# Moving the modulation sums of a hybrid layer kernel: second gate's sums into the experts' second product, one sum a level in the delta rule's inverse

## The reference, cut to what matters

```
mod = silu(c) @ w_ada + b_ada              # c: one row of 1024, w_ada: 1024 x 6144
shift1, scale1, gate1, shift2, scale2, gate2 = split(mod, 6)
h = rms_norm(x, norm1_gain) * (1 + scale1) + shift1
... h @ w_in, banded attention, convolution ...
# gated delta rule, per chunk of 64 tokens and head:
sol = triangular_solve(I + lower, rhs)     # unit lower triangular, here by its inverse
x = x + gate1 * (mix @ w_out)
h = rms_norm(x, norm2_gain) * (1 + scale2) + shift2
y = peer(h)     # 16384 one-neuron experts: gelu(h @ down), routed gates, (gates * act) @ up
x = x + gate2 * y
```

## Time and profile before

| | |
|---|---|
| median of 3 runs | 1708.43 us (1706.43 to 1713.17) |
| the profiled execution | 1703.49 us, its span 1701.8 us |
| PE busy | 1583.1 us, 93% |
| DVE busy | 1240.0 us, 73% |
| ACT busy | 899.9 us, 53% |
| granted PE clock, mean | 0.971 |
| DMA | 314.37 MB, mean 185 GB/s |

### The profile page before, as it was taken

The page is one execution under the profiler, slowest core; times in us unless marked ns, Lnnn a source line. Parts: engine busy times, 40 slices in busy tenths (PEclk is TensorE's granted clock), DMA queues, the critical chain, the costliest instruction groups (busy, mean ns, idle before and its releaser), DMA issues. The chain is left out here.

```text
span 1701.8 us, 26523 instructions
## 1 busy us (share of the span) xinstructions
PE 1583.1 (93%) x10358; PEld 1431.5 (84%) x10358; DVE 1240.0 (73%) x2494; ACT 899.9 (53%) x1497; POOL 45.6 (3%) x83
## 2 busy tenths in 40 slices
PE   5985789899999999999999999899999898989988
PEld 5975668899999999988888888797888677789977
DVE  5887777789997999956777766657886666654654
ACT  6763255455545555545555555556556746454443
POOL 0002300000000000000000000020000000000000
PEclk9997889999999999999999999999999899999999
DMA  9953446476766545557777767654443222545542
GB/s 327 336 178 96 150 169 197 134 238 225 227 210 224 167 145 167 157 194 249 243 245 247 240 237 242 209 174 149 142 153 127 73 76 100 173 148 174 188 156 102
DMA packets 110809, 314.37 MB, mean 185 GB/s; under 512 B 8465, under 2 KB 9057, under 8 KB 101217
## 3 DMA queue, kind: packets, MB, share of 16 engines
q1 hardware_dynamic: 98976, 276.94, 48.9%
q10 hardware_dynamic: 11040, 33.66, 5.8%
q0 software_dynamic: 672, 2.12, 0.4%
HBM read 293.80 MB, written 18.89 MB: 184 GB/s over the span
## 5 line engine op out<-in xcount | busy, mean ns | idle before, releaser
L300 PE MATMUL ps<-parts,parts 128*128 128x512 f32 (+1 forms) x4992 | 971.5, 356 | 27.2 <-DVE parts L290 21.0
L300 PEld LDWEIGHTS ps<-parts,parts 128*128 128x128 f32 x4992 | 824.6, 191 | 162.0 <-DVE parts L290 20.1
L285 ACT CAST parts<-lead 128x512 fp32r<-128x512 f32 x940 | 579.3, 620 | 624.6 <-PE ps L300 399.1
L290 DVE TENSOR_TENSOR parts<-lead,parts 128x512 fp32r<-128x512 f32 x940 | 641.1, 688 | 341.0 <-ACT parts L285 337.7
L1742 PE MATMUL ps<-parts,parts 128*128 128x256 f32 x3072 | 386.8, 285 | 4.5 <-DVE parts L290 4.5
L1742 PEld LDWEIGHTS ps<-parts,parts 128*128 128x128 f32 x3072 | 374.1, 192 | 5.5 <-DVE parts L290 5.5
L375 PE MATMUL ps<-lead,mem 128*128 128x128 f32 (+2 forms) x292 | 47.2, 328 | 50.7 <-ACT mem L491 25.9
L375 PEld LDWEIGHTS ps<-lead,mem 128*128 128x128 f32 (+2 forms) x292 | 41.4, 164 | 56.6 <-ACT mem L491 27.4
L1916 DVE TENSOR_SCALAR mem<-lead,mem 128x128 f32<-128x128 f32 x256 | 71.0, 339 | 0.0
L1728 PE MATMUL ps<-mem 128*128 128x128 f32 x512 | 67.8, 275 | 0.7 <-DVE mem L1916 0.7
L1728 PEld LDWEIGHTS ps<-mem 128*128 128x128 f32 x512 | 62.8, 192 | 1.1 <-issue 1.1
(11 more groups left out here) (339 smaller groups left out, 968.5 us busy)
## 6 DMA issues: line engine op xcount, KB each, us to landing
lead<-in_peer_expert_down SPq DMA_DIRECT2D x64, 1024.0 KB, 5.6
lead<-in_peer_expert_up SPq DMA_DIRECT2D x64, 1024.0 KB, 5.6
lead<-in_w_in SPq DMA_DIRECT2D x50, 1024.0 KB, 5.1
lead<-in_w_ffn_in SPq DMA_DIRECT2D x22, 1024.0 KB, 5.1
act_spill<-mem ACTq DMA_DIRECT2D x32, 512.0 KB, 5.1
mem<-act_spill ACTq DMA_DIRECT2D x32, 512.0 KB, 3.5
mem<-in_w_ada SPq DMA_DIRECT2D x27, 512.0 KB, 5.3
lead<-in_w_ffn_out SPq DMA_DIRECT2D x11, 1024.0 KB, 4.9
```

The costliest lines, as they stand in the source:

```text
L285: act.copy(w_hi[g % BUFFERS], st.words(n, u * UNIT, UNIT)).then_inc(hi_ready, 1)
L290: dve.tensor_tensor(w_lo[g % BUFFERS], st.words(n, u * UNIT, UNIT), w_hi[g % BUFFERS].bitcast(F32), ALU.subtract).then_inc(lo_ready, 1)
L300: mm = pe.matmul(o, lhs[a], rhs[b], start=start and i == 0, stop=stop and i == 2, skip_group_check=True, **kw)
```

## The change

Three things move.
- The second gate's eight sums leave the inverse, w_out and the query product. They are now made in the experts' second product, one behind unit 7 of each of the groups 20 to 27 (`late_mod`). Their tiles are loaded into pieces 4 to 11 of the gates: SP waits until `weights(11)` is done (`s_pr` 12) and then issues one tile behind every second weight piece (`load_late`). The columns' bias is added behind unit 228, and only then can POOL store the gate and load the row.
- The other 24 fills are dealt anew: two behind level 0 of the inverse as before, one behind each of levels 1 to 5, one behind the copy of line 1399, four in w_out.
- The bias, shift and scale of the second norm are formed in w_out, behind units 12 and 13.

The row silu(c) now lies in the place of the second gate's row (`gate2`), since it must last until group 27 and the gate's row comes after.

```diff
-        c_row = at(O_MODS + 3 * D, D)
+        c_row = gate2
...
-        FILL1, FILL2, FILL3, FILL4 = 9, 12, 25, 32
-        fill_tile = [f % FILLS if f < FILL3 else (f - FILL3) % (FILLS - 1) for f in range(FILL4)]
+        FILL1, FILL2, FILL3, FILL4 = 9, 12, 20, 24
+        fill_tile = [f % FILLS for f in range(FILL4)]
+        late_tiles = [at(O_R + (4 + i) * D, D) for i in range(KT)]
...
+        def load_late(sp, i):
+            sp.dma_start(late_tiles[i], A["w_ada"][(5 * KT + i) // 2][:, i % 2 * D:(i % 2 + 1) * D]).then_inc(s_late, 16)
+        def late_mod(dve, i):
+            if i == 0:
+                dve.wait_ge(s_late, 16 * KT)
+            v = late_tiles[i]
+            dve.scalar_tensor_tensor(out=v, in0=v, scalar=1.0, in1=c_row, op0=ALU.mult, op1=ALU.mult,
+                                     accum_out=mod_cols[:, 5 * KT + i:5 * KT + i + 1]).then_inc(s_mod, 1)
...
-                    fill_mods(dve, FILL2 + 2 * i, FILL2 + 2 * i + 2)
+                    fill_mods(dve, FILL2 + i + (i > 0), FILL2 + i + 2)
...
-                dve.wait_ge(s_mod, 3 * KT)
-                cols = mod_cols[:, 3 * KT:5 * KT]
-                dve.tensor_tensor(cols, cols, mod_bias[:, 3 * KT:5 * KT], ALU.add).then_inc(s_gate, 1)
-                dve.wait_ge(s_gain, 48)
-                dve.wait_ge(s_gate, 2)
-                dve.tensor_copy(norm_shift, cols[:, 0:KT])
-                dve.scalar_tensor_tensor(out=norm_scale, in0=cols[:, KT:2 * KT], scalar=1.0, in1=gain_cols[:, 1, :],
-                                         op0=ALU.add, op1=ALU.mult)
-                fill_mods(dve, FILL2 + 12, FILL3)
+                fill_mods(dve, FILL2 + 7, FILL3)
...
         def mods_beside_rows(dve, i):
             if i in (5, 7, 9, 11):
                 fill_mods(dve, FILL3 + (i - 5) // 2, FILL3 + (i - 3) // 2)
+            elif i == 12:
...
+                dve.tensor_tensor(cols, cols, mod_bias[:, 3 * KT:5 * KT], ALU.add).then_inc(s_gate, 1)
+            elif i == 13:
...
+                dve.tensor_copy(norm_shift, mod_cols[:, 3 * KT:4 * KT])
+                dve.scalar_tensor_tensor(out=norm_scale, in0=mod_cols[:, 4 * KT:5 * KT], scalar=1.0, in1=gain_cols[:, 1, :],
+                                         op0=ALU.add, op1=ALU.mult)
...
-                    if c and u == 1:
-                        fill_mods(dve, FILL4 - 4 + c, FILL4 - 3 + c)
-                    if c == 3 and u == 5:
-                        gates = mod_cols[:, 5 * KT:6 * KT]
-                        dve.wait_ge(s_mod, FILL4)
-                        dve.tensor_tensor(gates, gates, mod_bias[:, 5 * KT:6 * KT], ALU.add).then_inc(s_gate, 1)
...
+                st.issue(sp, n_up[0] + 24)
+                sp.wait_ge(s_pr, 12)
+                for i in range(KT):
+                    load_late(sp, i)
+                    st.issue(sp, n_up[0] + 26 + 2 * i)
                 st.issue(sp, n_in2a[0])
...
+                    if i % 8 == 7 and 20 <= q < 20 + KT:
+                        late_mod(dve, q - 20)
+                    if i == 8 * 28 + 4:
+                        gates = mod_cols[:, 5 * KT:6 * KT]
+                        dve.wait_ge(s_mod, 4 * KT)
+                        dve.tensor_tensor(gates, gates, mod_bias[:, 5 * KT:6 * KT], ALU.add).then_inc(s_gate, 1)
```

More of the change, by code:

```diff
@@ L422, in build @@
         fill_tiles = [at(o, D) for o in fill_at]
-        FILL1, FILL2, FILL3, FILL4 = 9, 12, 25, 32
-        fill_tile = [f % FILLS if f < FILL3 else (f - FILL3) % (FILLS - 1) for f in range(FILL4)]
+        FILL1, FILL2, FILL3, FILL4 = 9, 12, 20, 24
+        fill_tile = [f % FILLS for f in range(FILL4)]
+        late_tiles = [at(O_R + (4 + i) * D, D) for i in range(KT)]
         fill_before = [max((e for e in range(f) if fill_tile[e] == fill_tile[f]), default=None) for f in range(FILL4)]
+        s_late = lasting_sem("late_tiles_loaded")
         s_fill = [lasting_sem(f"fill_loaded{i}") for i in range(FILLS)]
@@ L1276, in _ @@
             def _(sp):
-                load_fills(sp, FILL2 + FILLS, FILL4 - 3)
+                load_fills(sp, FILL2 + FILLS, FILL4)
             @block.gpsimd
@@ L1521, in mods_beside_rows @@
                 fill_mods(dve, FILL3 + (i - 5) // 2, FILL3 + (i - 3) // 2)
+            elif i == 12:
+                cols = mod_cols[:, 3 * KT:5 * KT]
+                dve.wait_ge(s_mod, 3 * KT)
+                dve.tensor_tensor(cols, cols, mod_bias[:, 3 * KT:5 * KT], ALU.add).then_inc(s_gate, 1)
+            elif i == 13:
+                dve.wait_ge(s_gain, 48)
+                dve.wait_ge(s_gate, 2)
+                dve.tensor_copy(norm_shift, mod_cols[:, 3 * KT:4 * KT])
+                dve.scalar_tensor_tensor(out=norm_scale, in0=mod_cols[:, 4 * KT:5 * KT], scalar=1.0, in1=gain_cols[:, 1, :],
+                                         op0=ALU.add, op1=ALU.mult)
         rows_stage("w_out", n_wout, 4, n_query[0] + SLOTS, (x_hi, x_lo), add_mix, Turn("mix1", mix), sum_roots,
-                   last=lambda sp: load_fills(sp, FILL4 - 3, FILL4), beside=mods_beside_rows)
+                   beside=mods_beside_rows)
         first_sems = retired()
```

## The result

The changed kernel takes 1714.66 us (median of 12 runs, 1707.68 to 1719.2) where the kernel before takes 1709.28 us beside it (12 runs, 1704.3 to 1713.88): a ratio of 1.003 with an interval of [1.0016, 1.0044]. Run once more later it took 1717.3 us beside 1708.05, a ratio of 1.0052 [1.0032, 1.0073]. So it is slower by some 5 to 9 us, 0.3 to 0.5%. I had forecast 1.3 us faster; the two measurements leave no room for that, and 1714.66 lies outside my range. The profiled execution took 1715.11 us.

A forecast was written before the change was run, and what follows sets the result against it. PE, busy 93% of the span, was taken as the bound, with DVE's sums delaying it in the inverse. Only the inverse's 1.34 us counted, all other terms 0: 1708.43 - 1.34 = 1707.1 us, range 1702.5 to 1712.0 us.

The forecast's parts named there:

- The gate's row: Second product's end: storing the second gate and loading its row need some 20 of 38 us left; hidden, 0.
- the late loads: Second product: activations landing after 8.5 us beside tiles make PE wait 17.6 us in all, 1724.7 us; chance 0.05.
- the demand forecast: Second product: added tiles raise DMA traffic from 243 to some 290 GB/s, a share of 0.85; cost 0.
- The inverse: Inverse, levels 2 to 5: fewer sums between levels shorten them from 14.24 to 12.9 us, 1.34 us less.
- what is late next: Inverse: after the sums go, PE's own two products with ACT's copy between them, which no sum touches.
- level 2: Inverse: DVE is free before PE's results are ready, so the last subtraction starts 0.94 us earlier.
- levels 3 to 5: Inverse: each set to the trace's shortest level, 3.23 us, giving 0.27, 0.13 and 0 us less.
- w_out and the query: w_out and query product: added small instructions and removed sums are hidden beside PE; 0, bounds 0 and 3.5 us.
- The late sums: Second product: eight added DVE sums fit with 2.3 us to spare; 0, bounds 0 and 9.8 us.
- The start of the experts: Experts' start: the gate's store and row load go from here, but PE had no gap; 0.
- slower: Whole kernel: outcome slower by over 0.5%, from late loads and part of the late sums; chance 0.06.
- the same: Whole kernel: outcome within 0.5%, above 1699.9 and below 1717.0 us; chance 0.91.

The follow-up runs named there:

- Experiments one to three: Kernel before with second gate's store held back, 1.0039; changed kernel without that store, 1.0003; changed kernel storing it in 32-byte pieces, 1.0012.
- late store: Kernel before, with only POOL's store and load of the second gate held until unit 228 of the second product: 1715.43 us, ratio 1.0039.
- fillers, again: Second run of the changed kernel with 32-byte-piece store, one reordering copy and six idle PE products at the inverse's end: 1704.49 us, ratio 0.9976.
- short sums: Changed kernel with the seven sums behind the inverse's levels cut to 64 of 1024 columns: 1715.82 us, ratio 1.0045.
- fillers: Changed kernel with 32-byte-piece store, one reordering copy and six idle PE products at the inverse's end: 1704.96 us, ratio 0.9983.
- fillers alone: Kernel before with only six idle PE products, two ahead of each of three waits at the inverse's end: 1707.2 us, ratio 0.9992.
- store and copy: Changed kernel with the gate stored in 32-byte pieces and one DVE copy behind unit 246 reordering the row: 1707.64 us, ratio 0.9996.
- contiguous store: Changed kernel with the gate's columns stored in 128 pieces of 32 bytes and the row read in steps of eight: 1709.46 us, ratio 1.0012.
- bias behind 223: Changed kernel with the bias, and so the store, five units earlier, behind unit 223 in place of 228: 1714.44 us, ratio 1.0036.
- changed again: The changed kernel run a second time, unaltered, beside the kernel before: 1717.3 us, ratio 1.0052.
- more fillers: Changed kernel with 32-byte-piece store, reordering copy, six idle PE products and 23 more before, in and after the inverse: 1704.98 us, ratio 0.9982.

## Why the prediction was wrong

- **The gate's row** is the step that failed. It said: the store lands in at most 9.8 us, both need some 20 us, 38 are left, "Hidden, with 18 us to spare", and so it put the term at 0. The store did land in 10.0 us, and the row was there in time. What failed is that the step asked only whether the moved transfer is late. It did not ask what it does to the others. It held up a load on which DVE, and behind it PE, waits: 6.92 us in the profile, 5.21 of gap and 1.52 in the units behind it, at a lower clock, with 0.2 around. Experiments one to three show it: the store alone moved loses 0.4%, the store taken out or in pieces of 32 bytes gives it back.
- The trace of before showed the harm. From 315 to 322 us, beside the store at its old place, the DMA engines moved 32 GB/s, and the weight piece asked for at 314.36 took 12.4 us. The six weight pieces beside the store landed in 8.5 us in the median, while others landed in 5.2. I used this row twice, once for "PE had no gap" and once as the price of the late loads, and did not ask why the pieces were so slow there. At its old place the store met transfers that PE did not need for a while; at the new one it met the load with 0.6 us to spare.
- The rival of the late loads had the right wait (activations, line 1946, now 1961) and the right threshold, 6.3 us: in the five profiles with the gap, a load's landing time less the gap is 6.19 to 6.26 us (11.4 less 5.21 here, 12.5 less 6.31 with the late store), and a landing of 5.9 us in the middle of the second product (fillers, again) made no gap. Its cause was wrong. The tiles of w_ada, which it blamed, made the loads beside them land in up to 5.1 us instead of 3.1 to 3.4, and DVE waited up to 1.05 us; this cost PE nothing over 234 units, with the demand forecast (290 GB/s in that stretch). In the second profile of the changed kernel one of these loads took 6.4 us, and PE paused for 0.20 us, so the tiles stay just inside the limit.
- **The inverse**: -1.34 us forecast, -1.38 us by the subtractions. The mechanism was right, and so was what is late next: short sums gained nothing. That the two figures agree within 0.04 us is luck: level 2 gave 0.70 us and not 0.94, levels 3 to 5 gave 0.68 and not 0.40, since the shortest level is 3.13 us and not 3.23. What the step left out is that it is followed by products whose clock isn't given. Of 1.4 us, 0.2 reached w_out. With fillers it did reach it, in two profiles: 41.55 us, and 43.01 with a pause of 1.17, against 44.35 with fillers alone.
- The start of the levels: a sum beside POOL still takes 2.27 us, in this profile behind level 0 alone; in store and copy and in fillers the one behind level 1 takes 2.3 us too. It was no part of the forecast gain.
- **w_out and the query**: 0 forecast, -0.16 measured up to the 64 products, whose own +1.63 us come from the clock and are found in either kernel. Right.
- **The late sums**: 0 forecast, 0.2286 us a matmul against 0.2285. Right. Their pattern is the one worked out: a sum of 1.22 us, then a low part without idle time.

```profile
1055.62 1.22 DVE L457 SCALAR_TENSOR_TENSOR mem<-mem,lead 128x1024 f32<-128x1024 f32 x1
...
1056.77 0.69 DVE L290 TENSOR_TENSOR parts<-lead,parts 128x512 fp32r<-128x512 f32 x1
```

- The start of the experts: 0 forecast. The pieces no longer meet a store there. The 1452 products take 175.98 us with the store there and without it (contiguous store). Right.
- The chances: "slower" had 0.06 for two mechanisms, neither of them this one. The size, 0.3%, stays within the 0.5% that it called the same; the second measurement, 0.52%, is at its border.

## What to carry to other kernels

A transfer that is moved has two prices: whether it comes in time, and what it does to all others while it runs. Read the second from the stretch where it stands now, by the bytes moved there and the landings of its neighbours, not by its own bytes. A gain of one or two microseconds in a chain with short waits of the matrix engine was only had here when the clock behind it stayed up, so look at the granted clock of the stretch that follows. Before believing a difference between two single profiles, find the stretches that no changed instruction touches and see how much they differ.

## What the runs showed of the hardware that I had not expected

- A store of 4 KB in 1024 pieces of 4 bytes lands in 10 to 11 us and for 8 us all transfers together move 35 to 80 GB/s, at a share of busy DMA engines up to 0.96 (51, 46 and 39 GB/s in the mean of 8 us in the changed kernel, before with a late store, and bias behind 223). The same bytes in 128 pieces of 32 bytes land in 3.2 us. The Trainium skill (DMA: Bandwidth & Descriptors, section "Why small descriptors are slow (HBM only)") gives 32 bytes of metadata for each piece and a fixed few cycles as the penalty; an estimate by it is 1024 x 36 = 37 KB, 0.2 us at the 203 GB/s of the row before the hold-up and 1 us at 37. The trace shows far more: 6.8 us between the two forms of the store. What in the small pieces costs so much, their number or their four bytes, was not tried apart, nor was the same store issued by another engine than POOL, whose own instruction takes 0.95 us for the one form and 0.59 for the other.
- A load issued 7.9 us behind that store still landed after 12.5 us, and DVE waited 8.42 us for it: the backlog counts, not only the store.
- Two executions of one kernel (fillers, twice) reach level 0 at 174.05 and 177.66 us. They differ in the granted clock of 126 to 147 us (0.68 and 0.51), where 48 products take 6.02 and 10.47 us.
- With the new order of the inverse PE pauses in some executions, 100 products before the levels' end, for 0.34 to 1.44 us, and nothing in the trace releases it ("issue"). It was there in short sums, store and copy, changed again and fillers again (more fillers had two of 0.50 and 0.74 us at other places), and not in the first profile of the changed kernel nor of fillers. Its cause is open.
- A VectorE multiplication of 128 x 1024 with one operand read in steps of eight takes 2.0 to 2.1 us with another operand in the accumulation memory, where the plain one takes 1.22; a copy with the same steps takes 1.14.
